# Layer 0's last two convolved blocks by seven half products in place of eight, with two row additions and one copy moved forward

## The chip, the core and the metric

The kernel runs on one core of a Trainium2 chip. The metric is device microseconds (us) of one execution. One core has five engines that run side by side and wait for each other by semaphores: TensorE (PE in the rows; its weight loads are PEld), VectorE (DVE), ScalarE (ACT), GpSimd (POOL) and SyncE (SP), which here only issues loads and stores; its issuing queue is SPq in the rows. Matrix products land in PSUM (`ps` in the rows, four slots of two banks here), and everything else on the chip lies in SBUF (`arena`, `resid`, `ring`, `small` and others).

## What is computed

Two layers of a hybrid backbone on 256 context and 512 latent tokens of width 1024. A layer mixes tokens (a bidirectional state-space scan, differential attention and latent attention share one input projection) and then runs 16 experts. The case touches the input projection of the scan in layer 0:

```python
for l in range(DEPTH):
    mod_l = split((silu_c @ ada_w[l] + ada_b[l]), N_MOD)
    h_l = modulate(rmsnorm(x, norm_mix_pre[l]), mod_l[0], mod_l[1])
    ...
    z, xbc, dt = split(h @ w_in, ...)       # xbc: 768 channels, six blocks of 128
    xbc = silu(centred_dwconv(xbc, conv_w, conv_b))           # 3 taps over tokens
    xs, bm, cm = split(xbc, [512, 640])     # blocks 0-3, block 4, block 5
    ...
    x = x + mod_l[5] * rmsnorm(expert_choice_ffn(...), norm_ffn_post[l])
```

`ada_w` gives rows of modulation. `xbc` has 768 channels, six blocks of 128: blocks 0 to 3 are `xs`, block 4 is `bm`, block 5 is `cm`. All is float32. Tokens number 768 in layer 0; in layer 1 block 5 is needed for the 512 latent tokens only.

## The kernel before

The program is written out engine by engine. `hT` holds the normed input, transposed: 8 slices of 128 features by 768 tokens. The six convolved blocks (`m` = 0 to 5) are made with channels on partitions, in PSUM jobs `conv_job(l, m)`.

**Plain blocks** (4 and 5): `feature_major` (lines 2468 to 2478; its products are L2476 in the rows) does 8 matmuls over the 8 feature slices for the first 512 tokens and 8 for the last 256. That is four half products each: two halves of the features by two halves of the tokens.

**Paired blocks** (0 with 1 and 2 with 3 in memory order of weights; pair `p` makes blocks `p` and `2 + p`): two blocks, two feature halves and two token halves are a 2 by 2 product of 2 by 2 blocks, done with seven half products in place of eight (`half_product`, lines 2861 to 2866, L2865 in the rows). One half product is four matmuls of 128 by 384. VectorE makes the sums that feed them: of tokens (`TH`), of weights (`SW`), and of the products, which it adds from PSUM into `E1`, `U3` and `CM` (`half_sum`, L1881; L1912 and L1933 are the sums that also free a PSUM slot). A product written twice into the same half bank must wait until its first value has been read: ScalarE copies it (`E1[p]`, L1304).

A float32 matmul shows as two records, so a half product is `x8` in the rows.

**Convolution.** For each block, in the order `CONV_ORDER = (2, 0, 3, 1, 4, 5)`, ScalarE scales by the middle tap and adds the bias (L1323, semaphore `conv_mid`), VectorE adds the two other taps with four instructions (L1987), and ScalarE applies SiLU (L1329, semaphore `xbc_ready`). Each engine takes the blocks strictly in that order. VectorE waits for all six before it multiplies block 4 by block 5 (L2002), and behind that product it copies the cumulative sums out of PSUM (L2007, L2008), which frees PSUM slot 3.

**TensorE after the paired blocks** (lines 2891 to 2920): block 4, the modulation rows `block_rows(l, 2, 2)` (L2508, 8 matmuls with the load of weights block 14), block 5, cumulative sums (L2900 to L2902), `block_rows(l, 2, 3)`, the turned sums `acT` (L2913, L2916), and then the gate product `z0` (L2923), whose PSUM slot is slot 3.

**Modulation rows.** `block_rows` leaves one block of 512 columns in PSUM; `rows_added` (line 1609) adds it to the rows so far and frees the slot: `rows_added(l, 2, 1)` stood behind convolved block 1, `rows_added(l, 2, 2)` behind block 4.

**Loads.** SyncE loads weight blocks of up to 2 MB into a ring of four slots, block `b` into slot `b % 4`. Its order is written out in line 822, and each load waits for the last use of the block that was in the slot (`block_used`, line 788):

```python
for b in [*range(10), 11, 10, 12, 13, 15, 14, *range(16, PRE_BLOCKS)]:
    ...
    if b >= RING and not (l and b - RING in EARLY):
        block_used(l, b - RING)
```

Block 10 has the weights of convolved blocks 0 to 3, block 15 those of blocks 4 and 5, blocks 12, 13, 14 and 16 the modulation rows `b` = 0 to 3 of part 2, block 17 those of the gate. For block 10, `block_used` waits until the last half product of the pairs is in PSUM (lines 804 to 810). Block 14 goes into the slot of block 10, so it is issued then. `block_rows(l, 2, 2)` waits for it (`arrived`, line 2463; semaphore `ring_full2`).

## Time and profile before

| | us |
|---|---|
| median of 3 runs | 2095.02 |
| lowest and highest of them | 2092.53, 2096.34 |
| the profiled execution, its own time | 2094.3 |
| its span, first to last instruction | 2092.2 |
| PE busy in it | 1942.3 (93%) |
| DVE, ACT, POOL busy | 721.6, 519.1, 186.9 |
| granted TensorE clock, mean | 0.988 of full speed |
| read from and written to HBM | 528.95 MB |

The profiled execution is 0.7 us below the median of the runs. Layer 0 mixes tokens until about 600 us of the span and runs its experts until about 1110 us; layer 1 does the same until about 1580 us and until the end. The six convolved blocks of layer 0 are made between 305 and 371 us. PE's busy time is modelled from its records and overlaps a little from row to row, so lengths of a stretch are best taken from start to start.

### The profile page before, as it was taken

Reading aid. Unit: us, or ns where it says so; the run is one execution under the profiler, and the core shown is the slowest. Engines: PE = TensorE matmul, PEld = TensorE weight load, DVE = VectorE, ACT = ScalarE, POOL = GpSimd, SP = SyncE. Lnnn points to the kernel's source line nnn. Section 1 sums busy time; section 2 is a strip of 40 time slices with the busy share of each in tenths; the row PEclk is TensorE's granted clock in tenths of the full one; section 3 lists DMA queues with packets and bytes.
Section 4 is the critical chain, followed back from the end, with each engine's and each line's share of the span. In section 5 each row is a group of like instructions: output and inputs, shape, how many; then the busy total and the mean of one; then the engine's idle time right before and its main releaser. Section 6 shows DMA issues by size and latency. Waiting matters only on the chain. (4 is left out here: it accounts for less than half of the span.)

```text
span 2092.2 us, 25952 instructions
## 1 busy us (share of the span) xinstructions
PE 1942.3 (93%) x10858; PEld 934.4 (45%) x10858; DVE 721.6 (34%) x1335; ACT 519.1 (25%) x1020; POOL 186.9 (9%) x216
## 2 busy tenths in 40 slices
PE   5998999989989999999999999999898998888886
PEld 2656565544433333333334866655445333232222
DVE  2258565372431110111113476563624111111113
ACT  4146552452300000000003255524321100000012
POOL 1300000120011111212012000001100000000000
PEclk9999999999999999999999999999999999999999
DMA  9520304222289999999999223024419999999996
GB/s 351 147 81 1 141 1 152 90 105 96 82 343 401 393 399 395 394 401 393 402 395 301 111 82 141 1 90 153 165 61 357 395 408 408 408 409 409 409 409 261
DMA packets 164805, 530.64 MB, mean 254 GB/s; under 512 B 11016, under 2 KB 19538, under 8 KB 164690
## 3 DMA queue, kind: packets, MB, share of 16 engines
q1 hardware_dynamic: 149344, 489.49, 60.0%
q0 software_dynamic: 15120, 39.43, 6.1%
q8 instruction: 87, 1.43, 0.3%
q14 instruction: 28, 0.23, 0.0%
q10 hardware_dynamic: 226, 0.07, 0.0%
HBM read 507.98 MB, written 20.97 MB: 253 GB/s over the span
## 5 line engine op out<-in xcount | busy, mean ns | idle before, releaser
L3267 PE MATMUL ps<-ring,arena 128*64 128x512 f32 x1040 | 233.2, 597 | 13.6 <-DMA ring<-in_w_up 8.8
L3267 PE MATMUL ps<-arena 128*64 128x512 f32 x720 | 165.0, 604 | 3.6 <-DMA arena<-in_w_gate 3.2
L3267 PEld LDWEIGHTS ps<-ring,arena 128*64 128x64 f32 x1040 | 72.1, 137 | 161.6 <-issue 141.3
L3093 PE MATMUL ps<-ring,arena 128*128 128x512 f32 x320 | 141.6, 597 | 1.0 <-ACT arena L1442 0.6
L2366 DVE TENSOR_TENSOR arena<-arena,ps 128x512 f32<-128x512 f32 x32 | 22.0, 688 | 280.1 <-ACT arena L1487 280.1
L3316 PE MATMUL ps<-ring,arena 128*64 128x512 f32 x496 | 112.4, 596 | 5.8 <-DMA ring<-in_w_down 5.8
L2476 PE MATMUL ps<-arena,ring 128*128 128x256 f32 (+1 forms) x384 | 110.4, 447 | 2.5 <-DMA ring<-in_w_in 2.5
L1487 ACT ACTIVATE arena<-ps 128x512 f32<-128x512 f32 x32 | 19.1, 597 | 373.4 <-PE ps L3267 373.4
L3316 PE MATMUL ps<-arena 128*64 128x512 f32 x432 | 97.9, 595 | 5.2 <-DMA arena<-in_w_down 4.5
L1066 ACT ACTIVATE arena<-ps 128x768 f32<-128x768 f32 (+6 forms) x111 | 79.9, 724 | 88.0 <-PE ps L2494 45.3
L3267 PEld LDWEIGHTS ps<-arena 128*64 128x64 f32 x720 | 50.4, 139 | 107.0 <-issue 100.3
L2476 PEld LDWEIGHTS ps<-arena,ring 128*128 128x128 f32 x384 | 73.2, 191 | 41.1 <-issue 31.5
L3093 PEld LDWEIGHTS ps<-ring,arena 128*128 128x128 f32 x320 | 59.7, 191 | 70.3 <-issue 69.5
L3216 PE MATMUL ps<-ring,arena 128*32 128x512 f32 x624 | 86.0, 594 | 0.4 <-DVE arena L2160 0.4
L2494 PE MATMUL ps<-const,arena 128*128 128x128 f32 x524 | 77.0, 283 | 7.9 <-DVE arena L1832 5.5
L1196 ACT ACTIVATE arena<-ps,nmax 128x768 f32<-128x768 f32 (+1 forms) x80 | 64.5, 811 | 60.6 <-DVE nmax L1715 56.1
L1715 DVE TENSOR_REDUCE nmax<-ps 128x1 f32<-128x768 f32 (+1 forms) x80 | 64.3, 846 | 39.8 <-PE ps L2682 38.9
L2494 PEld LDWEIGHTS ps<-const,arena 128*128 128x128 f32 x524 | 58.4, 143 | 42.5 <-issue 23.9
L2312 DVE TENSOR_TENSOR arena<-arena,ps 64x512 f32<-64x512 f32 x16 | 11.1, 692 | 188.7 <-ACT arena L1483 188.7
L2156 DVE TENSOR_TENSOR arena<-ps,coef 128x512 f32<-128x512 f32 (+1 forms) x48 | 28.8, 600 | 128.0 <-PE ps L3192 127.4
L3316 PEld LDWEIGHTS ps<-ring,arena 128*64 128x64 f32 x496 | 34.2, 137 | 77.3 <-issue 72.0
L914 POOL DMA_INDIRECT arena<-normed_rows,small x32 | 33.3, 1039 | 394.2 <-PE ps L3192 356.9
(417 smaller groups left out, 2821.8 us busy)
## 6 DMA issues: line engine op xcount, KB each, us to landing
ring<-in_w_up SPq DMA_DIRECT2D x33, 2048.0 KB, 14.7
ring<-in_w_gate SPq DMA_DIRECT2D x32, 2048.0 KB, 21.1
ring<-in_w_down SPq DMA_DIRECT2D x30, 2048.0 KB, 23.0
ring<-in_ada_w SPq DMA_DIRECT2D x24, 2048.0 KB, 9.9
arena<-in_w_down SPq DMA_DIRECT2D x19, 2048.0 KB, 23.2
arena<-in_w_gate SPq DMA_DIRECT2D x18, 2048.0 KB, 22.5
arena<-in_w_up SPq DMA_DIRECT2D x12, 2048.0 KB, 13.6
ring<-in_w_in SPq DMA_DIRECT2D x6, 2048.0 KB, 14.0
```

Of the source, the lines that this page charges most:

```text
L914: pool.indirect_dma_start(got_l[e % 2], None, halves_in, at_rows(e, 0)).then_inc(got_lat[e % 2], 16)
L1066: act.activation(dst, src, func, scale=scale).then_inc(*J.free(j))
L1196: act.activation(by_halves(PD[u % 2][m], t, nk // 2), by_halves(J.tile(j), t, 512), ACT.Exp, bias=nmax[:, c:c + 1], accum_out=esum[:, c:c ...
L1715: dve.tensor_reduce(nmax[:, c:c + 1], by_halves(J.tile(j), t, 512), AX_X if t < CT else AX_XY, ALU.max, negate=True).then_inc(S["negmax"], 1)
L2156: TT(x4, src.rearrange("p (c h n) -> p c h n", h=parts, n=n), cF[:, :, s].rearrange("p (h c) -> p c h", h=parts).unsqueeze(3) .to_broadcas ...
L2366: TT(hid_l, hid_l, px[0][:, 512:1024], ALU.mult).then_inc(S["hid_lat"], 1)
L2476: ins = mm(o[0:n, c0:c1], w[:, k, col:col + n], hT[:, k, c0:c1], start=k == 0, stop=k == KD - 1)
L2494: ins = pe.transpose(o[:, k * P:(k + 1) * P], src(k), ident)
L3093: ins = mm(o[:, hf * 512:(hf + 1) * 512], mix, wo[hf][:, k, :], start=k == 0, stop=k == KD - 1)
L3216: ins = mm(px[1][32 * i:32 * i + 32, 0:512], xc[e % 2][:, at:at + CAP_C], w[c][:, hf * 512:hf * 512 + 512], start=b + c == 0, stop=b * c == 3)
L3267: ins = mm(px[0][hf * 64:hf * 64 + 64, col:col + 512], xl[e % 2][:, at:at + CAP_L], w[c][:, hf * 512:hf * 512 + 512], start=b + c == 0, st ...
L3316: ins = mm(px[1][hf * 64:hf * 64 + 64, 512:1024], hT_l[0][:, at:at + CAP_L], w[c][:, hf * 512:hf * 512 + 512], start=b + c == 0, stop=b * ...
```

## The change

In layer 0 alone, blocks 4 and 5 are made as a third pair, by seven half products (`bc_product`). `CONV_ORDER` becomes a list per layer: in layer 0 block 5 now comes before block 4. VectorE makes four sums of weights (`bc_weight_sums`, before the last sum of block 1's pair) and seven sums of products (`bc_halves`, before the taps of block 5). ScalarE copies the first product (`E1[0]`) ahead of its work on block 1. TensorE does the first half product, then `block_rows(l, 2, 2)`, and then the other six. `rows_added(l, 2, 1)` moves forward to before the pairs' last sums in both layers, and in layer 0 `rows_added(l, 2, 2)` into `bc_halves`. SyncE's order stays as it was. The semaphore counts follow (33 sums and 15 products per layer).

```diff
@@ layout
-        CONV_ORDER = (2, 0, 3, 1, 4, 5)
+        CM += [CM[0], CM[2]]
+        CONV_ORDER = ((2, 0, 3, 1, 5, 4), (2, 0, 3, 1, 4, 5))
+        def last_pair_of_channels(x):
+            return SW[1 + x // 2][:, :, P * (x % 2):P * (x % 2) + P]
+        def plain(l, m):
+            return l > 0 and m >= 4
@@ ScalarE
+                    if l == 0 and m == 1:
+                        act.wait_ge(S["half_products"], products0 + 11)
+                        act.activation(E1[0], J.tile(conv_job(l, 4))[:, 0:HT], ACT.Copy).then_inc(S["half_out"], 1)
...
+                    elif m == 5:
+                        act.wait_ge(S["half_sums"], sums0 + 31)
                     else:
-                        act.wait_ge(*J.filled(j))
+                        act.wait_ge(*J.freed(conv_job(l, 5 if m == 4 else 2 * m + 1)))
@@ VectorE
+                rows_added(l, 2, 1)
                 early_half(0)
                 last_half(0)
+                def bc_weight_sums():
+                    n15 = block_base(l) + 15
+                    dve.wait_ge(ring_full[n15 % RING], ring_turns(n15) * 16)
+                    wb15, s_ = ringv(n15), [last_pair_of_channels(x) for x in range(4)]
+                    dve.wait_ge(*J.filled(conv_job(l, 2)))
+                    half_sum(s_[0], wb15[:, 0:4, P:2 * P], wb15[:, 4:8, P:2 * P], ALU.add)
+                    sums_done(21)
+                    half_sum(s_[1], s_[0], wb15[:, 0:4, 0:P], ALU.subtract)
+                    sums_done(22)
+                    half_sum(s_[2], wb15[:, 0:4, 0:P], wb15[:, 0:4, P:2 * P], ALU.subtract)
+                    half_sum(s_[3], wb15[:, 4:8, 0:P], s_[1], ALU.subtract)
+                def bc_halves():
+                    j0, j1 = conv_job(l, 4), conv_job(l, 5)
+                    dve.wait_ge(S["half_out"], out0 + 3)
+                    rows_added(l, 2, 2)
+                    dve.wait_ge(S["half_products"], products0 + 12)
+                    half_sum(CM[4][:, 0:HT], E1[0], J.tile(j0)[:, 0:HT], ALU.add)
+                    dve.wait_ge(S["half_products"], products0 + 13)
+                    half_sum(E1[0], E1[0], J.tile(j0)[:, 512:512 + HT], ALU.add)
+                    sums_done(28)
+                    dve.wait_ge(*J.filled(j0))
+                    TT(U3[0], E1[0], J.tile(j0)[:, 512:512 + HT], ALU.add).then_inc(*J.free(j0))
+                    dve.wait_ge(*J.freed(j0))
+                    half_sum(CM[5][:, HT:TOK], U3[0], J.tile(j1)[:, 0:HT], ALU.add)
+                    half_sum(E1[0], E1[0], J.tile(j1)[:, 0:HT], ALU.add)
+                    dve.wait_ge(S["half_products"], products0 + 15)
+                    half_sum(CM[5][:, 0:HT], U3[0], J.tile(j1)[:, 512:512 + HT], ALU.add)
+                    sums_done(30)
+                    dve.wait_ge(*J.filled(j1))
+                    TT(CM[4][:, HT:TOK], E1[0], J.tile(j1)[:, 0:HT], ALU.add).then_inc(*J.free(j1))
-                for m in CONV_ORDER:
+                for m in CONV_ORDER[l]:
...
                     if m == 3:
                         early_half(1)
+                        if l == 0:
+                            bc_weight_sums()
                         last_half(1)
+                    if m == 5 and l == 0:
+                        bc_halves()
...
-                    if m in (1, 4):
-                        rows_added(l, 2, m // 2 + (m == 1))
+                    if l and m == 4:
+                        rows_added(l, 2, 2)
@@ TensorE
                 w = arrived(wb + 15)
-                feature_major(conv_job(l, 4), w, 0, P)
-                block_rows(l, 2, 2)
-                feature_major(conv_job(l, 5), w, P, P, conv_start(l, 5) // P)
+                if l:
...
+                else:
+                    pe.wait_ge(*J.empty(conv_job(l, 4)))
+                    bc_product(0, 0, w[:, 0:4, 0:P], rows_half(0, 0)).then_inc(S["half_products"], 1)
+                    block_rows(l, 2, 2)
+                    pe.wait_ge(S["half_out"], out0 + 3)
+                    bc_product(0, 0, w[:, 4:8, 0:P], rows_half(4, 0)).then_inc(S["half_products"], 1)
+                    pe.wait_ge(S["half_sums"], sums0 + 24)
+                    bc_product(0, 1, last_pair_of_channels(1), TH[1]).then_inc(S["half_products"], 1)
+                    pe.wait_ge(*J.empty(conv_job(l, 5)))
+                    bc_product(1, 0, last_pair_of_channels(0), TH[0]).then_inc(S["half_products"], 1)
+                    pe.wait_ge(S["half_sums"], sums0 + 28)
+                    bc_product(0, 1, last_pair_of_channels(2), TH[2]).then_inc(*J.fill(conv_job(l, 4)))
+                    bc_product(1, 1, w[:, 4:8, P:2 * P], TH[3]).then_inc(S["half_products"], 1)
+                    pe.wait_ge(S["half_sums"], sums0 + 30)
+                    bc_product(1, 0, last_pair_of_channels(3), rows_half(4, 1)).then_inc(*J.fill(conv_job(l, 5)))
```

TensorE in layer 0, behind the last half product of the second pair, before the change (the row of 128x384 with `half_sums` ahead of it is that product; `ring,silu_c` rows are modulation rows; brackets name the semaphores waited for):

```order
L2865 MATMUL ps<-arena 128x384 [waits half_sums]
L2865 MATMUL ps<-arena 128x384 x3
L2476 MATMUL ps<-arena,ring 128x512 [waits ps_free0,ring_full3]
L2476 MATMUL ps<-arena,ring 128x512 x7
L2476 MATMUL ps<-arena,ring 128x256 x8
L2508 MATMUL ps<-ring,silu_c 32x512 [waits ring_full2,ps_free1]
L2508 MATMUL ps<-ring,silu_c 32x512 x7
L2476 MATMUL ps<-arena,ring 128x512 [waits ps_free2]
L2476 MATMUL ps<-arena,ring 128x512 x7
L2476 MATMUL ps<-arena,ring 128x256 x8
L2900 MATMUL ps<-small,const 128x48 [waits ps_free3,la_ready]
```

The same place with the change:

```order
L2954 MATMUL ps<-arena,ring 128x384 [waits ps_free0,ring_full3]
L2954 MATMUL ps<-arena,ring 128x384 x3
L2561 MATMUL ps<-ring,silu_c 32x512 [waits ring_full2,ps_free1]
L2561 MATMUL ps<-ring,silu_c 32x512 x7
L2954 MATMUL ps<-arena,ring 128x384 [waits half_out]
L2954 MATMUL ps<-arena,ring 128x384 x3
L2954 MATMUL ps<-arena 128x384 [waits half_sums]
L2954 MATMUL ps<-arena 128x384 x3
L2954 MATMUL ps<-arena 128x384 [waits ps_free2]
L2954 MATMUL ps<-arena 128x384 x3
L2954 MATMUL ps<-resid,arena 128x384 [waits half_sums]
L2954 MATMUL ps<-resid,arena 128x384 x3
```

The modulation rows of block 14 (`ring_full2`) now stand behind four matmuls of 128x384 where they stood behind sixteen, and six half products stand behind them.

VectorE from its last sum of products to the copies that free PSUM slot 3, with the change (`conv_mid` is ScalarE's middle tap; `xbc_ready` its last SiLU):

```order
L2021 TENSOR_TENSOR arena<-arena,ps 128x384 [waits ps_full2,half_sums]
L2040 SCALAR_TENSOR_TENSOR resid<-arena,par,resid 128x255 [waits conv_mid]
L2040 SCALAR_TENSOR_TENSOR resid<-arena,par,resid 128x511
L2040 SCALAR_TENSOR_TENSOR resid<-arena,par,resid 128x255 [waits dve_step]
L2040 SCALAR_TENSOR_TENSOR resid<-arena,par,resid 128x511
L2040 SCALAR_TENSOR_TENSOR resid<-arena,par,resid 128x255 [waits conv_mid]
L2040 SCALAR_TENSOR_TENSOR resid<-arena,par,resid 128x511
L2040 SCALAR_TENSOR_TENSOR resid<-arena,par,resid 128x255 [waits dve_step]
L2040 SCALAR_TENSOR_TENSOR resid<-arena,par,resid 128x511
L1632 TENSOR_TENSOR mod_rows<-ps,mod_rows 128x512 [waits half_used,ps_free1]
L2055 TENSOR_TENSOR arena<-resid 128x768 [waits xbc_ready]
L2060 COPY small<-ps 128x6x8 [waits ps_full3]
```

Before the change the taps of the last block alone stood between the last product and `xbc_ready`:

```order
L1615 TENSOR_TENSOR mod_rows<-ps,mod_rows 128x512 [waits ps_full1,ps_free1]
L1987 SCALAR_TENSOR_TENSOR resid<-ps,par,resid 128x255 [waits conv_mid]
L1987 SCALAR_TENSOR_TENSOR resid<-ps,par,resid 128x511
L1987 SCALAR_TENSOR_TENSOR resid<-ps,par,resid 128x255 [waits dve_step]
L1987 SCALAR_TENSOR_TENSOR resid<-ps,par,resid 128x511
L1618 TENSOR_TENSOR mod_rows<-ps,mod_rows 128x512 [waits half_used,ps_free1]
L2002 TENSOR_TENSOR arena<-resid 128x768 [waits xbc_ready]
L2007 COPY small<-ps 128x6x8 [waits ps_full3]
```

A last sum and the taps of a second block have come in ahead of the last block's taps.

ScalarE at the copy of the first product, with the change:

```order
L1337 ACTIVATE resid<-arena,par 128x768 [waits half_sums]
L1343 ACTIVATE resid<-resid 128x768 [waits half_sums]
L1326 ACTIVATE arena<-ps 128x384 [waits half_products]
L1337 ACTIVATE resid<-resid,par 128x768 [waits ps_free3]
L1343 ACTIVATE resid<-resid 128x768 [waits half_sums]
```

The copy stands behind the SiLU of block 3, which waits for that block's taps (`half_sums`), and ahead of block 1's middle tap.

## Rows read from the trace of the kernel before

**Rows 1.** Whole stages: us, PE busy, PEld, DVE, ACT, POOL busy, PEclk, DMA share, GB/s.

```profile
386.00:600.00 214.00, 198.85 (x963) 99.20 (x964) 105.16 (x208) 74.83 (x148) 26.31 (x33) 1.00 0.29 109
600.00:1110.00 510.00, 508.07 (x3564) 181.57 (x3566) 69.78 (x123) 38.13 (x61) 76.03 (x57) 1.00 1.02 393
1110.00:1580.00 470.00, 445.03 (x2491) 278.14 (x2490) 245.14 (x411) 192.06 (x385) 35.59 (x49) 0.98 0.33 120
1580.00:2093.00 513.00, 447.50 (x1889) 161.52 (x1887) 105.52 (x203) 51.86 (x88) 15.44 (x17) 0.98 0.98 389
```

**Rows 2.** PE's waits in layer 0's experts, 600 to 1110: total us, times, longest.

```profile
PE ps L3306 <- DVE arena L2366: 1.0, 1, 1.0
PE ps L3316 <- ACT arena L1517: 0.7, 1, 0.7
```

**Rows 3.** Timeline of PE, 330 to 400: start us, us, ..., [idle before <- releaser].

```profile
341.33 2.74 PE L2865 MATMUL ps<-arena 128*128 128x384 f32 x8
343.91 10.48 PE L2476 MATMUL ps<-arena,ring 128*128 128x512 f32 x32
354.32 1.92 PE L2508 MATMUL ps<-ring,silu_c 128*32 128x512 f32 x16
356.18 10.59 PE L2476 MATMUL ps<-arena,ring 128*128 128x512 f32 x32
366.60 0.32 PE L2900 MATMUL ps<-small,const 128*128 128x48 f32 x2
...
373.19 1.13 PE L2923 MATMUL ps<-ring,arena 128*128 128x512 f32 x2
```

**Rows 4.** Timeline of SyncE's DMA issues, 330 to 400.

```profile
344.10 0.99 SPq L835 DMA_DIRECT2D ring<-in_ada_w  x2
345.14 3.42 SPq L835 DMA_DIRECT2D ring<-in_w_in  x1
```

**Rows 5.** The load issued at 344.10, alone: from issue to landing.

```profile
DMA to landing us min/median/max: 7.8/7.8/7.8
```

**Rows 6.** Timeline of VectorE, 330 to 400.

```profile
343.31 0.55 DVE L1881 TENSOR_TENSOR arena<-arena,ps 128x384 f32<-128x384 f32 x1
...
345.22 2.33 DVE L1987 SCALAR_TENSOR_TENSOR resid<-arena,par,resid 128x255 f32<-128x255 f32 x4 [0.48 <-ACT resid L1323]
...
367.83 2.31 DVE L1987 SCALAR_TENSOR_TENSOR resid<-ps,par,resid 128x255 f32<-128x255 f32 x4 [9.46 <-ACT resid L1323]
...
371.05 0.96 DVE L2002 TENSOR_TENSOR arena<-resid 128x768 f32<-128x768 f32 x1 [0.31 <-ACT resid L1329]
...
372.16 0.25 DVE L2008 COPY small<-ps 128x96 f32<-128x96 f32 x1
...
387.31 3.70 DVE L2023 TENSOR_TENSOR arena<-arena 128x512 f32<-128x512 f32 x6
```

**Rows 7.** Timeline of ScalarE, 330 to 400.

```profile
347.57 0.84 ACT L1329 ACTIVATE resid<-resid 128x768 f32<-128x768 f32 x1 [2.39 <-DVE resid L1987]
...
366.80 0.99 ACT L1323 ACTIVATE resid<-ps,par 128x768 f32<-128x768 f32 x1 [8.15 <-PE ps L2476]
370.18 0.84 ACT L1329 ACTIVATE resid<-resid 128x768 f32<-128x768 f32 x1 [2.38 <-DVE resid L1987]
```

**Rows 8.** Timeline of ScalarE, 300 to 332: a copy of half a product.

```profile
308.60 0.49 ACT L1304 ACTIVATE arena<-ps 128x384 f32<-128x384 f32 x1 [4.44 <-PE ps L2865]
```

**Rows 9.** Timeline of PE, 10 to 30: row-block products after waits for their loads.

```profile
18.96 3.52 PE L2508 MATMUL ps<-ring,silu_c 128*32 128x512 f32 x16 [6.06 <-DMA ring<-in_ada_w]
24.39 1.92 PE L2508 MATMUL ps<-ring,silu_c 128*32 128x512 f32 x16 [1.91 <-DMA ring<-in_ada_w]
```

**Rows 10.** Timeline of PE, 386 to 620 and 1425 to 1530: the longer waits.

```profile
589.96 0.40 PE L3176 MATMUL ps<-const,arena 32*128 32x32 f32 x4 [2.33 <-ACT arena L1468]
...
1450.75 1.14 PE L2971 MATMUL ps<-resid 32*128 32x512 f32 x8 [2.13 <-issue]
```

**Rows 11.** The 8 us behind that last wait, columns as in rows 1.

```profile
1452.00:1460.00 8.00, 8.00 (x32) 4.91 (x36) 4.54 (x5) 2.46 (x3) 2.08 (x2) 0.57 0.00 0
```

More of the change, by code:

```diff
@@ L1300, in _ @@
                     act.wait_ge(s_xst, 16 * nq)
-                products0, sums0 = 10 * l, 22 * l
+                products0, sums0 = 15 * l, 33 * l
                 for p in range(2):
@@ L1312, in _ @@
                 act.activation(dts[1], dts[1], ACT.Ln).then_inc(S["dt_log"], 1)
-                for i, m in enumerate(CONV_ORDER):
+                for i, m in enumerate(CONV_ORDER[l]):
                     j = conv_job(l, m)
-                    if m in (2, 3):
+                    if l == 0 and m == 1:
+                        act.wait_ge(S["half_products"], products0 + 11)
+                        act.activation(E1[0], J.tile(conv_job(l, 4))[:, 0:HT], ACT.Copy).then_inc(S["half_out"], 1)
+                    if plain(l, m):
+                        act.wait_ge(*J.filled(j))
+                    elif m in (2, 3):
                         act.wait_ge(S["half_sums"], sums0 + (15, 20)[m - 2])
-                    elif m < 2:
-                        act.wait_ge(*J.freed(conv_job(l, 2 * m + 1)))
+                    elif m == 5:
+                        act.wait_ge(S["half_sums"], sums0 + 31)
                     else:
-                        act.wait_ge(*J.filled(j))
+                        act.wait_ge(*J.freed(conv_job(l, 5 if m == 4 else 2 * m + 1)))
                     on = slice(conv_start(l, m), TOK)
-                    src = CM[m] if m < 4 else J.tile(j)
+                    src = J.tile(j) if plain(l, m) else CM[m]
                     act.activation(XB[:, m, on], src[:, on], ACT.Identity, bias=pc[:, R_CB + m:R_CB + m + 1],
                                    scale=pc[:, R_CW + CONV_T + m:R_CW + CONV_T + m + 1]).then_inc(S["conv_mid"], 1)
-                    if m < 4:
-                        act.wait_ge(S["half_sums"], sums0 + (16, 19, 21, 22)[i])
+                    if not plain(l, m):
+                        act.wait_ge(S["half_sums"], sums0 + (16, 19, 25, 26, 32, 33)[i] - (0 if l == 0 or i < 2 else 4))
                     else:
@@ L1865, in _ @@
                     dve.wait_ge(s_xst, 16 * nq)
[L1866 removed]
+                sums0, out0, products0 = 33 * l, 3 * l, 15 * l
                 n10 = block_base(l) + 10
@@ L1979, in _ @@
                         early_half(1)
+                        if l == 0:
+                            bc_weight_sums()
                         last_half(1)
+                    if m == 5 and l == 0:
+                        bc_halves()
                     dve.wait_ge(*v.next(S["conv_mid"]))
-                    src, dst = CM[m] if m < 4 else J.tile(j), XB[:, m, :]
+                    src, dst = J.tile(j) if plain(l, m) else CM[m], XB[:, m, :]
                     for tap, sh in ((0, -1), (2, 1)):
@@ L1991, in _ @@
                             dve.wait_ge(*v.next(dve_step))
-                    if m < 4:
+                    if not plain(l, m):
                         ins.then_inc(S["half_sums"], 1)
@@ L2850, in _ @@
                 w = arrived(wb + 10)
-                sums0, out0 = 22 * l, 2 * l
+                sums0, out0 = 33 * l, 3 * l
                 def weight(p, half, k0):
@@ L2891, in _, with bc_product @@
                 w = arrived(wb + 15)
-                feature_major(conv_job(l, 4), w, 0, P)
-                block_rows(l, 2, 2)
-                feature_major(conv_job(l, 5), w, P, P, conv_start(l, 5) // P)
+                if l:
+                    feature_major(conv_job(l, 4), w, 0, P)
+                    block_rows(l, 2, 2)
+                    feature_major(conv_job(l, 5), w, P, P, conv_start(l, 5) // P)
+                else:
+                    def bc_product(i, hf, a, b):
+                        o = J.tile(conv_job(l, 4 + i))[:, 512 * hf:512 * hf + HT]
+                        for k in range(4):
+                            ins = mm(o, a[:, k, :], b[:, k, :], start=k == 0, stop=k == 3)
+                        return ins
+                    pe.wait_ge(*J.empty(conv_job(l, 4)))
+                    bc_product(0, 0, w[:, 0:4, 0:P], rows_half(0, 0)).then_inc(S["half_products"], 1)
+                    block_rows(l, 2, 2)
+                    pe.wait_ge(S["half_out"], out0 + 3)
[9 more added lines that the diff above has]
+                    bc_product(1, 0, last_pair_of_channels(3), rows_half(4, 1)).then_inc(*J.fill(conv_job(l, 5)))
                 pe.wait_ge(*w_.next(S["la_ready"]))
```

1 line of the change is left out of this document (removed).

## The prediction

> **What bounds the kernel.** I read the table of stages first. From 600 to 1110 us, layer 0's experts, PE is busy 508 of 510 us [rows 1], and its two longest waits there are 1.0 and 0.7 us, for VectorE and ScalarE, none for a load [rows 2]: PE bounds that stage. While layer 0 mixes, from 386 to 600, PE is busy 199 of 214 us with the DMA engines at 0.29 [rows 1], so PE and its short waits for its neighbours bound that one too. Layer 1 mixes in the same way, and its experts have the DMA engines at 0.98 [rows 1]. Every load of the later stages waits for a slot that PE frees, so a shift of PE in layer 0 moves the loads behind it as well. I found no place behind 387 us that waits for something earlier than PE's own work, and so take it that what PE gains or loses here reaches the end in full.
>
> Then the timelines of PE, SyncE, VectorE and ScalarE around the blocks. PE goes through the stretch without a gap: the last half product of the pairs from 341.33 to 343.91, block 4 to 354.32, modulation rows to 356.18, block 5 to 366.60, and small products until the gate product at 373.19 [rows 3].
>
> **What is saved.** A half product takes 2.58 us (341.33 to 343.91). Blocks 4 and 5 took 10.41 and 10.42 us, 20.83 together [rows 3]. Seven half products take 7 x 2.58 = 18.06. PE does **2.8 us** less work, all of it on the path.
>
> **The load.** Where PE now does the modulation rows decides more. They begin at 354.32 today, behind sixteen matmuls. With the change they stand behind one half product, so PE comes to them at 343.91 + 2.58 = 346.49. They need weights block 14, and SyncE issues it when the pairs' last product is done, at 344.10 [rows 4], into the slot that this product's weights had. It lands 7.8 us after its issue [rows 5], at 351.9. The change leaves SyncE's order and that condition alone. Today the load has 2.4 us to spare; with the change PE stands idle from 346.5 to 351.9, **5.4 us**, and the six other half products are queued behind.
>
> **The copy and the weight sums** are hidden by that same wait. Four sums of 128x512 on VectorE cost 0.62 us each by the rows of 128x512 (six in 3.70, [rows 6]), 2.5 us together. They come ahead of block 3's taps, which move from 345.22 to about 343.31 + 0.48 + 2.5 + 0.47 = 346.8. Those take 2.33, ScalarE's SiLU 0.84 [rows 6, 7], the copy 0.49 [rows 8]: the copy ends at about 350.4, 1.5 us before the load lands. Without the load's wait, PE would stand until 350.4 in place of 346.49 + 1.86 = 348.35: 2.0 us. The other sums of `bc_halves` (0.5 us each, by 343.31) fall each beside a half product of 2.58 us and hold nobody, nor do the two additions of modulation rows: the first falls into idle time of VectorE, and the second has its product long before its slot is wanted.
>
> **The tail.** PE ends its seventh product at 351.9 + 1.86 + 6 x 2.58 = 369.2, against 366.60: 2.6 us later (5.4 less 2.8). Today the chain behind block 5 is middle tap at 366.80 (0.99), VectorE's taps (2.31), SiLU at 370.18, the product at 371.05 and the copies to 372.16 + 0.25 = 372.4 [rows 6, 7]. That frees the slot for the gate product at 373.19, 0.8 us early. With the change the last product completes block 4, and VectorE, which goes in order, does the last sum (0.55), block 5's taps (2.31), ScalarE block 5's SiLU (0.84) and only then block 4's middle tap; from there all is as before. The chain is 0.55 + 2.31 + 0.84 = 3.7 us longer. Less the 0.8 us that it had to spare, PE waits **2.9 us** ahead of the gate product.
>
> Everything behind waits for PE's gate product, eight microseconds long. The sum without the clock is 5.4 - 2.8 + 2.9 = **+5.5 us**.
>
> **The clock.** The granted clock is 1.00 in all of layer 0 from 386 on [rows 1]; both new waits could take it to the lower of its levels, 1.2 in place of 2.4 GHz. The rows have cases on both sides. The same sixteen records of modulation rows took 3.52 us after a wait of 6.06 us for their load and 1.92 after one of 1.91 [rows 9]: 1.6 us lost. A wait of 2.33 us at 589.96 left the clock at 1.00 through its stage, one of 2.13 us at 1450.75 was followed by 8 us at 0.57 [rows 10, 11], 8 x 0.43 = 3.4 us lost. So each wait can cost 0 to 3.4 us. The first, of 5.4 us, is nearest to the 6.06 and the same work follows: I take 1.6. The second, 2.9 us, lies between: I take half of that, 0.8. The Trainium skill ("TensorE: Matmul & The Clock Gate", Part 1: The HAM clock gate) says that the low clock is the default and that activity releases it, so that a gap brings it back; it speaks against this change. By the page the sum would be 5.5 + 1.6 + 0.8 = 7.9, without it 5.5; rows 9 agree with it.
>
> The sum is **+7.9 us**: 2094.3 + 7.9 = 2102.2 for an execution like the profiled one. That one lies 0.7 below the median of the runs, so I expect a median of **2103 us**, 0.4% slower.
>
> **The rivals.** A measurement of this kernel tells 0.2%, 4.2 us, from no change.
>
> (a) *The load does not bind.* If block 14 is there earlier than its row says, the copy binds in its place from 350.4: PE loses 2.0, saves 2.8, and waits 2.9 at the gate: +2.1 us, about 2097, no change that can be told. For it speaks that three loads of 2 MB are issued together and this one's 7.8 us could be shorter alone; against it that it was issued first. It decides from a landing before 348.5. Chance 0.08.
>
> (b) *The saving shows, on the other side.* One mechanism: VectorE's and ScalarE's tail is hidden behind the small products and the gate waits for nobody. It would need the load before 346.5, and the last SiLU to start by about 368.2 where its present start is 370.18, so that slot 3 is free for PE at 370.4. Then PE's 2.8 us reach the end: 2092 us, not slower. Against it stand the order on VectorE and the issue at 344.10. Chance 0.03.
>
> (c) *Given back later.* PE waits a good 15 us between 386 and 600 [rows 1]. If some of these waits end on engines or loads that the shift does not move, they shrink, and of 5.5 us 2 or 3 remain: 2097 to 2098. For it speaks that 15 us are a lot; against it that GpSimd, ScalarE and VectorE there work on what PE has just made. Chance 0.10.
>
> (d) *The clock falls for long at both waits*, 3.4 us each: 5.5 + 6.8 = +12.3, 2107. Chance 0.07, slower as well.
>
> (e) *It does not do what it says*: a count that makes the plain path run on, or an order of waits that costs a lot more than 10 us. The written order of PE shows the seven products. Chance 0.02.
>
> The forecast itself, +4.2 to +10, has 0.70.
>
> **How the numbers follow.** Slower by over 0.2%: forecast 0.70, (d) 0.07 and half of (e), 0.78. Within 0.2%: (a), most of (c) and most of (b), 0.20. Faster by over 0.2%: the saving is 2.8 us, so it would need something that I do not see, 0.02. The range begins at 2097.5, which takes in most of (c) and the forecast without any loss of clock less the scatter of the runs (they lie 2.5 us below to 1.3 above their median); it ends at 2107.5 with (d).
>
> **What would show it.** In PE's timeline of the changed kernel: one half product at 344, then a wait of 5 to 5.5 us for the load into `ring` ahead of the modulation rows at about 352, which take nearer 3.5 than 1.9 us; the copy on ScalarE at about 350, before that; six half products without a gap; then the gate product at about 379 to 381 behind a wait of about 3 us for VectorE's copies. From there to the end every landmark is later by one and the same 6 to 9 us. The prediction is wrong if the modulation rows begin before 350, if the gate product begins before 376, or if the shift at the start of the experts is much smaller than at the gate product.

## The result, and the profile after

| | before | after |
|---|---|---|
| median, us (runs) | 2095.42 (8) | 2104.78 (8) |
| lowest to highest, us | 2092.53 to 2097.60 | 2101.83 to 2109.03 |
| ratio after to before, 95% interval | | 1.0048 (1.0039 to 1.0058) |
| profiled execution, us; its span | 2094.3; 2092.2 | 2102.89; 2100.8 |
| mean granted clock over the runs of after | | 0.985 |

The change makes the kernel slower by 0.48% (0.39 to 0.58%); between the medians it is 9.4 us, or 0.45%. (Here and below the ratio with its interval is an estimate from all the runs, and can differ from the quotient of the two medians by up to 0.0004.) The forecast was 2103, range 2097.5 to 2107.5.

The timeline of TensorE in the profile of after, 330 to 405 us (columns as in rows 3; `L2954` is `bc_product`, `L2561` `block_rows`, `L2999` the gate product):

```profile
340.86 2.74 PE L2918 MATMUL ps<-arena 128*128 128x384 f32 x8
343.44 2.74 PE L2954 MATMUL ps<-arena,ring 128*128 128x384 f32 x8
351.67 3.61 PE L2561 MATMUL ps<-ring,silu_c 128*32 128x512 f32 x16 [5.49 <-DMA ring<-in_ada_w]
355.21 2.85 PE L2954 MATMUL ps<-arena,ring 128*128 128x384 f32 x8
357.89 5.32 PE L2954 MATMUL ps<-arena 128*128 128x384 f32 x16
363.06 2.74 PE L2954 MATMUL ps<-resid,arena 128*128 128x384 f32 x8
365.63 2.74 PE L2954 MATMUL ps<-arena,ring 128*128 128x384 f32 x8
368.21 2.74 PE L2954 MATMUL ps<-arena 128*128 128x384 f32 x8
370.80 0.32 PE L2976 MATMUL ps<-small,const 128*128 128x48 f32 x2
...
380.43 1.10 PE L2999 MATMUL ps<-ring,arena 128*128 128x512 f32 x2 [2.98 <-DVE small L2061]
```

Where rows 3 have no gap, two waits stand: 5.49 us for the load ahead of the modulation rows, and 2.98 us for VectorE's copies ahead of the gate product. The seven half products are there and take 2.58 us each from start to start, but for the one behind the modulation rows (2.68). The modulation rows take 3.61 us in place of 1.92.

The load was issued at the same place as before. SyncE's issue, and that load alone from issue to landing:

```profile
343.63 0.99 SPq L844 DMA_DIRECT2D ring<-in_ada_w  x2
```

```profile
DMA to landing us min/median/max: 7.9/7.9/7.9
```

343.63 + 7.9 = 351.5, and the modulation rows begin at 351.67. Their other condition, the PSUM slot that the moved addition frees (semaphore `ps_free1`), was met long before, at 333.5:

```profile
332.78 0.68 DVE L1629 TENSOR_TENSOR mod_rows<-ps,mod_rows 128x512 f32<-128x512 f32 x1
```

ScalarE in the same stretch (the copy of the first product is L1326, the middle tap L1337, SiLU L1343):

```profile
348.78 0.84 ACT L1343 ACTIVATE resid<-resid 128x768 f32<-128x768 f32 x1 [4.05 <-DVE resid L2040]
349.53 0.47 ACT L1326 ACTIVATE arena<-ps 128x384 f32<-128x384 f32 x1
...
374.64 1.02 ACT L1337 ACTIVATE resid<-arena,par 128x768 f32<-128x768 f32 x1
378.05 0.84 ACT L1343 ACTIVATE resid<-resid 128x768 f32<-128x768 f32 x1 [2.39 <-DVE resid L2040]
```

VectorE: one of the four weight sums, then the tail, from the last sum (L2021) over the taps of blocks 5 and 4 (L2040) to the copies that free slot 3:

```profile
343.31 0.68 DVE L1895 TENSOR_TENSOR arena<-ring 128x512 f32<-128x512 f32 x1
...
371.06 0.56 DVE L2021 TENSOR_TENSOR arena<-arena,ps 128x384 f32<-128x384 f32 x1 [2.09 <-PE ps L2954]
371.54 2.32 DVE L2040 SCALAR_TENSOR_TENSOR resid<-arena,par,resid 128x255 f32<-128x255 f32 x4
375.69 2.33 DVE L2040 SCALAR_TENSOR_TENSOR resid<-arena,par,resid 128x255 f32<-128x255 f32 x4 [1.83 <-ACT resid L1337]
...
380.03 0.25 DVE L2061 COPY small<-ps 128x96 f32<-128x96 f32 x1
```

The copy ends at 350.0, 1.5 us before the load has landed. From the end of TensorE's last half product (370.80) to the end of the copies (380.28) it is 9.5 us; before it was 5.8 (366.60 to 372.41, [rows 3, 6]). The difference is the 3.7 us of a sum, a block's taps and a SiLU.

Later landmarks. Execution by execution the whole program lies a little earlier or later already at 340 us, so I count from the first product behind the second pair: 343.91 before [rows 3], 343.44 after. The gate product lies 29.28 us behind it before and 36.99 after: **+7.7 us**. The experts of layer 0 begin at 601.66 before, and here:

```profile
478.14 0.60 PE L3206 MATMUL ps<-arena,const 16*128 16x32 f32 x2 [1.92 <-ACT arena L1441]
...
609.96 7.09 PE L3343 MATMUL ps<-ring,arena 128*64 128x512 f32 x32 [0.21 <-DVE arena L2213]
```

That is 257.75 before and 266.52 after, +8.8 us. The 1.1 us that came in between has its place behind 478 us, after a wait of 1.92 us:

```profile
348.00:356.00 8.00, 4.33 (x19) 1.20 (x20) 3.60 (x7) 2.98 (x4) 0.00 (x0) 0.57 1.05 391
...
476.00:484.00 8.00, 6.08 (x26) 4.33 (x23) 2.11 (x4) 2.16 (x6) 3.25 (x6) 0.79 1.02 409
```

(Stretches of the profile of after, columns as in rows 1.) The granted clock is 0.57 around the wait for the load and 0.79 in the later stretch, where the profile of before stood at 1.00: in 348 to 356 by its own row of that stretch, and from 386 on by rows 1.

### The profile page after: what moved, and what is told of

Its sections match the earlier page's. It is cut to its first block and busy times, and to the rows that moved or that the text cites. A ratio compares the mean times of both kernels' runs of the same rounds, so it can differ in the third digit from the quotient of the medians.

```text
span 2100.8 us, 25951 instructions
## 1 busy us (share of the span) xinstructions
PE 1945.5 (93%) x10850; PEld 934.3 (44%) x10850; DVE 727.8 (35%) x1346; ACT 520.1 (25%) x1021; POOL 187.4 (9%) x216
## 5 line engine op out<-in xcount | busy, mean ns | idle before, releaser
L2529 PE MATMUL ps<-arena,ring 128*128 128x256 f32 (+1 forms) x320 | 89.1, 438 | 2.2 <-DMA ring<-in_w_in 2.2
L2529 PEld LDWEIGHTS ps<-arena,ring 128*128 128x128 f32 x320 | 61.2, 192 | 31.1 <-issue 22.2
```

The costliest lines, as they stand in the source:

```text
L2529: ins = mm(o[0:n, c0:c1], w[:, k, col:col + n], hT[:, k, c0:c1], start=k == 0, stop=k == KD - 1)
```

## The experiments

The theory: the loss is a wait for a load whose issue the change did not move, a longer chain of taps behind the last product, and a clock that falls in these waits. The rivals: the copy or the weight sums hold PE and not the load; the moved additions cost something; the clock plays no part; the scheme of seven products costs this much in any order.

Each set of runs had runs of the kernel before on the same chip. "Gate product" is its distance from the first product behind the second pair in the profiled execution, against the 29.28 us of before; "experts" is the same for the start of layer 0's experts, against 257.75. (In e2, whose rows come first, both are counted from the end of the pairs, 342.12.) "Clock" is the mean granted clock over the executions; before's was 0.9883 beside e2 to e5, 0.9876 beside e1 and e6 to e8, and 0.9875 beside e9 to e11.

| kernel | gate product, us | experts, us | time of this, before, us | ratio (95%) | clock |
|---|---|---|---|---|---|
| the change | +7.7 | +8.8 | 2104.78, 2095.42 | 1.0048 (1.0039 to 1.0058) | 0.9848 |
| e1_additions | 0.0 | +2.5 | 2096.72, 2095.81 | 1.0001 (0.9991 to 1.0010) | 0.9875 |
| e2_rows_first | +10.0 | +15.3 | 2107.21, 2094.64 | 1.0063 (1.0046 to 1.0080) | 0.9842 |
| e3_rows_later | +6.1 | +13.1 | 2110.29, 2094.64 | 1.0078 (1.0061 to 1.0094) | 0.9812 |
| e4_early_copy | +7.8 | +9.2 | 2107.74, 2094.64 | 1.0066 (1.0049 to 1.0083) | 0.9840 |
| e5_filled | +6.0 | +9.3 | 2104.51, 2094.64 | 1.0051 (1.0034 to 1.0068) | 0.9865 |
| e6_early_sums_out | +5.4 | +6.1 | 2098.89, 2095.81 | 1.0013 (1.0003 to 1.0023) | 0.9868 |
| e7_no_waits | +0.5 | +6.0 | 2100.74, 2095.81 | 1.0024 (1.0015 to 1.0034) | 0.9851 |
| e8_no_waits_sums_out | -2.6 | -1.1 | 2094.57, 2095.81 | 0.9995 (0.9986 to 1.0004) | 0.9865 |
| e9_filled_gate | +0.5 | +2.3 | 2098.28, 2095.85 | 1.0011 (1.0002 to 1.0020) | 0.9872 |
| e10_no_waits_sums_out | -2.6 | +1.7 | 2095.18, 2095.85 | 0.9993 (0.9984 to 1.0002) | 0.9860 |
| e11_both_filled | +6.1 | +9.8 | 2102.49, 2095.85 | 1.0029 (1.0018 to 1.0040) | 0.9876 |

**e1, the moved addition alone.** The kernel before with

```diff
+                rows_added(l, 2, 1)
                 early_half(0)
...
-                    if m in (1, 4):
-                        rows_added(l, 2, m // 2 + (m == 1))
+                    if m == 4:
+                        rows_added(l, 2, 2)
```

> The kernel before, with the addition of modulation rows (2, 1) moved forward in both layers and nothing else. Theory: it falls into idle time of VectorE (0.5 us, then 2 us more behind the next sum), so 0 within the scatter, and the gate product of layer 0 begins when it did. Rival (a moved addition holds up the pairs' last sums and through them PE): up to +1.4 us, 0.7 a layer.

No difference, in the time or at the gate product: where it was moved to, the addition is free. But its profiled execution has two stretches at a lower clock further on, and so begins the experts 2.5 us later than before's, though nothing else was changed:

```profile
432.00:440.00 8.00, 6.58 (x29) 3.03 (x29) 6.29 (x9) 4.00 (x7) 2.04 (x2) 0.79 0.01 2
472.00:480.00 8.00, 7.78 (x25) 5.17 (x26) 1.92 (x2) 0.28 (x2) 1.39 (x3) 0.79 1.02 408
```

The profiled execution of before has 1.00 in both. So what a single profile gains or loses between the gate product and the experts can be scatter, by 2.5 us at least; the profiles are compared below at the gate product.

**e2, the rows first, without a third pair.** The kernel before with the modulation rows ahead of plain block 4, in layer 0:

```diff
+                if l == 0:
+                    block_rows(l, 2, 2)
                 feature_major(conv_job(l, 4), w, 0, P)
-                block_rows(l, 2, 2)
+                if l:
+                    block_rows(l, 2, 2)
```

> The kernel before, with the modulation rows of block 14 put ahead of plain block 4 in layer 0 and nothing else. Theory (the load's issue at 344.1 and its 7.8 us set when the rows can begin): PE stands idle about 8 us from the end of the pairs, the rows begin at about 352, and every later landmark moves by +8 us, and by 1 to 3.4 us more if the clock falls: +8 to +11. Rival (the wait of the change is for ScalarE's copy or VectorE's sums, not for the load): neither exists here, so no wait and no change of time, 0.

TensorE in it, SyncE's issue of the load and its landing, and VectorE's addition of the modulation rows before:

```profile
350.61 3.56 PE L2508 MATMUL ps<-ring,silu_c 128*32 128x512 f32 x16 [8.33 <-DVE mod_rows L1615]
```

```profile
342.31 0.99 SPq L835 DMA_DIRECT2D ring<-in_ada_w  x2
```

```profile
DMA to landing us min/median/max: 8.1/8.1/8.1
```

```profile
349.83 0.68 DVE L1615 TENSOR_TENSOR mod_rows<-ps,mod_rows 128x512 f32<-128x512 f32 x1
```

The pairs end at 342.1, the load is issued at 342.31 and lands at 350.4, and PE begins at 350.61. But the row names VectorE's addition as what ended the wait, and rightly: it frees the PSUM slot that the rows need, it still stands behind block 1's taps here, and it ends at 350.51. The two conditions are met within 0.1 us of each other, so e2 cannot tell them apart and does not show the load's wait by itself. It refutes its rival, since with no copy and no weight sum in it the kernel waits 8.3 us. It also shows what the moved addition is for. At its old place it holds the rows as long as the load does here, and in the change it would have held them longer: block 1's taps end there at 353.3, so that by my estimate (no run has it) the addition would have ended at about 353.9, 2.4 us behind the load.

The kernel loses 10.0 us at the gate product: the wait and 1.6 us in the modulation rows, which take 3.56. That is within the 8 to 11 expected, but the whole time rose by 12.6, beyond it.

**e4, the copy earlier.** The change with the copy moved ahead of block 3's SiLU, behind its middle tap:

```diff
-                    if l == 0 and m == 1:
-                        act.wait_ge(S["half_products"], products0 + 11)
-                        act.activation(E1[0], J.tile(conv_job(l, 4))[:, 0:HT], ACT.Copy).then_inc(S["half_out"], 1)
                     if plain(l, m):
...
                                    scale=pc[:, R_CW + CONV_T + m:R_CW + CONV_T + m + 1]).then_inc(S["conv_mid"], 1)
+                    if l == 0 and m == 3:
+                        act.wait_ge(S["half_products"], products0 + 11)
+                        act.activation(E1[0], J.tile(conv_job(l, 4))[:, 0:HT], ACT.Copy).then_inc(S["half_out"], 1)
```

> The change, with the copy of the first product ahead of block 3's SiLU on ScalarE, so that it ends at about 346.9 in place of 350.0. Theory (the load binds until 351.7, the copy is hidden): no gain, rows still begin at 351.7, +8 to +9.5 us against before as the change. Rival (the copy binds): the time falls by 3 us, to +6.

ScalarE's copy and TensorE's modulation rows:

```profile
346.59 0.49 ACT L1338 ACTIVATE arena<-ps 128x384 f32<-128x384 f32 x1 [1.50 <-PE ps L2954]
```

```profile
351.95 3.64 PE L2561 MATMUL ps<-ring,silu_c 128*32 128x512 f32 x16 [5.40 <-DMA ring<-in_ada_w]
```

The copy is there 4.9 us before the rows begin, and nothing is gained: +7.8 at the gate product. The time is +13.1 us, where +8 to +9.5 was expected; its interval overlaps the change's (1.0049 to 1.0083, 1.0039 to 1.0058) and excludes the rival's +6. The copy does not bind beside the load. Why the median lies 3.7 us above the change's is not shown; its profiled execution is the fastest of its four and has, as the change's, falls of the clock in layer 0 at the load's wait and near 478 alone.

**e3, the rows later.** The change with the modulation rows behind the third half product and their addition one sum later:

```diff
                     bc_product(0, 0, w[:, 0:4, 0:P], rows_half(0, 0)).then_inc(S["half_products"], 1)
-                    block_rows(l, 2, 2)
...
                     bc_product(0, 1, last_pair_of_channels(1), TH[1]).then_inc(S["half_products"], 1)
+                    block_rows(l, 2, 2)
```

> The change, with the modulation rows two half products later (behind the third) and their addition on VectorE one sum later. Theory: the load no longer binds; PE goes through one product and then waits until the copy ends at about 350.0 (3.9 us), has the load when it comes to the rows, and ends the seventh product at about 367.4 in place of 370.8; the wait of 3.0 us before the gate product stays. Against before: +4.2 us without a fall of the clock, up to +6 with one. Rival (the load is not the cause, the seven products with their sums cost this much anyway): the same +9 us as the change.

TensorE in it:

```profile
351.93 4.31 PE L2954 MATMUL ps<-arena,ring 128*128 128x384 f32 x8 [3.86 <-ACT arena L1326]
...
380.65 1.10 PE L2999 MATMUL ps<-ring,arena 128*128 128x512 f32 x2 [2.97 <-DVE small L2061]
381.73 1.59 PE L2999 MATMUL ps<-ring,arena 128*128 128x512 f32 x2
383.39 2.06 PE L2999 MATMUL ps<-ring,arena 128*128 128x512 f32 x2
```

The wait for the load is gone and the next one shows, the 3.86 us for the copy that I had worked out. But the clock fell in both places (4.31 us for a half product of 2.74, 2.06 for matmuls of 1.10): +6.1 at the gate product where +4.2 was expected without a fall. The whole time missed by far: +15.7 us where up to +6 was expected. The mean clock of its executions is the lowest of all. Beyond its two waits the profile shows the lower clock in three more places between the gate product and the experts (from about 444, 481 and 604 us). At the experts it is +13.1, so 7.0 us came in on that stretch. This says where the time went; why this kernel falls most often stays open.

**e5, the wait filled.** The change with two half products of no use while the load is awaited, written where the third product overwrites them:

```diff
+                    for _ in range(2):
+                        bc_product(0, 1, w[:, 0:4, 0:P], rows_half(0, 0))
                     block_rows(l, 2, 2)
```

> The change, with two more half products of no use (the first product's operands, into a half bank that the third product overwrites) while PE waits for the load. It adds 5.2 us of work to PE. Theory (PE stands idle for the load, and the idle time also takes the clock down): the rows begin at the same 351.7, now after a wait of 0.3 us, the clock stays at 1.00, the rows take 1.9 in place of 3.6 us and all behind is 1.9 us earlier: +6 to +7 against before. Rival (the clock plays no part): the same +9. Rival (PE was not idle there): 5 us slower than the change.

TensorE in it:

```profile
343.87 7.90 PE L2954 MATMUL ps<-arena,ring 128*128 128x384 f32 x24
352.10 1.92 PE L2561 MATMUL ps<-ring,silu_c 128*32 128x512 f32 x16 [0.33 <-DMA ring<-in_ada_w]
...
379.16 1.10 PE L3001 MATMUL ps<-ring,arena 128*128 128x512 f32 x2 [2.97 <-DVE small L2061]
380.29 2.05 PE L3001 MATMUL ps<-ring,arena 128*128 128x512 f32 x2
```

With 5.2 us more work on PE the rows begin at the same distance, take 1.92 us, and the gate product is 1.7 us earlier than in the change. So PE was idle, and the idle time itself cost 1.7 us of clock. Then the clock falls behind the second wait, which in the change's profiled execution it did not. In the time it does not show: +9.9 against the +6 to +7 expected, and against the change's +9.4. The second wait, still open here, is filled in e11.

**e6, the sums out earlier.** The change with the copies of the cumulative sums ahead of block 4's taps in layer 0:

```diff
                     if m == 5 and l == 0:
                         bc_halves()
+                    if m == 4 and l == 0:
+                        sums_out()
...
+                if l:
+                    sums_out()
                 j = jb("cum")
-                dve.wait_ge(*J.filled(j))
...
```

> The change, with VectorE's copies of the cumulative sums (which free PSUM slot 3) ahead of block 4's taps in layer 0, where they stood behind the last SiLU. Theory (the tail holds PE by that slot): the wait of 3.0 us ahead of the gate product is gone, the gate product begins at about 377.3 in place of 380.4, 3 us less than the change at every later landmark: +5 to +6.5 against before. Rival (PE, or what follows, waits for the last SiLU in another place): the 3 us come back behind the gate product, no gain, +8 to +9.

TensorE's modulation rows, the end of the seven products and the gate product, in its timeline, and the landing of the load, which was issued at 345.25:

```profile
353.79 3.64 PE L2569 MATMUL ps<-ring,silu_c 128*32 128x512 f32 x16 [5.99 <-DMA ring<-in_ada_w]
...
370.58 2.74 PE L2962 MATMUL ps<-arena 128*128 128x384 f32 x8
...
379.75 1.13 PE L3007 MATMUL ps<-ring,arena 128*128 128x512 f32 x2
```

```profile
DMA to landing us min/median/max: 8.4/8.4/8.4
```

The wait of 3 us is gone; PE comes to the gate product straight from the turned sums. It is 2.3 us nearer than in the change, because this execution's load landed 0.5 us later (a wait of 5.99). One small one takes its place: between the first two pairs of matmuls of the gate product PE now waits for VectorE's last addition of modulation rows, which stands behind block 4's taps, so that the second pair starts 1.54 us behind the first where before it was 1.10. That gives 0.4 us back. The late landing also tells what the rows wait for: here they begin 0.1 us behind it (345.25 + 8.4 = 353.65, 353.79), and in the change, e4 and e5, with landings at 351.5, 351.8 and 352.0, they begin at 351.67, 351.95 and 352.10. The rows move with the load.

The time is +3.1 where +5 to +6.5 was expected: 6.3 us came back and not 3. The mean clock rose with it (0.9868 against 0.9848). In the profiled executions the clock had not fallen at this wait in the change, so these two profiles do not show where the other 3 us were.

**e7, no wait within the seven products.** The modulation rows behind the first four products and their addition as in e3, the copy as in e4, and the fourth product, which needs no copy, second:

```diff
                     bc_product(0, 0, w[:, 0:4, 0:P], rows_half(0, 0)).then_inc(S["half_products"], 1)
+                    pe.wait_ge(S["half_sums"], sums0 + 21)
+                    pe.wait_ge(*J.empty(conv_job(l, 5)))
+                    bc_product(1, 0, last_pair_of_channels(0), TH[0]).then_inc(S["half_products"], 1)
...
```

> The change, with three moves: the fourth product second (it needs no copy), the modulation rows behind the first four products, the copy ahead of block 3's SiLU. Theory: no wait of PE from 343 to the end of the seven products, which come at about 363.4 in place of 370.8; the 3.0 us ahead of the gate product stay, since the tail of taps is as long as before: gate product 0.3 us later than in the kernel before, +0.3 us, no difference that can be measured. Rival (without the waits the saving of 2.8 us shows): -2.8.

The last of the products and the gate product:

```profile
361.51 2.74 PE L2954 MATMUL ps<-arena 128*128 128x384 f32 x8
...
373.74 2.04 PE L3000 MATMUL ps<-ring,arena 128*128 128x512 f32 x2 [2.99 <-DVE small L2061]
375.86 1.75 PE L3000 MATMUL ps<-ring,arena 128*128 128x512 f32 x2
```

From 343.98 to 364.1 PE has no gap, and the gate product lies at +0.5 (expected +0.3). What the seven products save, the longer tail takes back. The time is +4.9 and not +0.3. The profiled execution shows where its own 6.0 us at the experts came in: 1.7 at the gate product, which runs at the lower clock, 2.6 behind the wait at 473 and 1.2 behind the one at 595.

**e9, the gate's wait filled.** e7 with one useless half product inside the 3.0 us, into the slot that the turned sums then overwrite:

```diff
+                    if l == 0 and at == 8:
+                        for k in range(4):
+                            mm(o[:, 0:HT], hT[:, k, 0:P], hT[:, k, 0:HT], start=k == 0, stop=k == 3)
                     for t in range(NT):
```

> The kernel of e7_no_waits with one half product of no use on PE ahead of the second set of turned sums (into a slot that they overwrite), inside the 3.0 us in which PE waits before the gate product. Theory (that wait itself costs 0.5 us, and what e7 lost beyond it is the clock that falls behind the wait): the gate product begins at the same distance from the first product as in e7 (29.8 us), after a wait of 0.4 us, runs at the full clock, and the time is 1.6 to 3 us below e7's: +2 to +3.5 against before. Rival (the rest of e7's loss has its cause elsewhere): the same +4.9.

```profile
367.47 2.85 PE L2988 MATMUL ps<-arena 128*128 128x384 f32 x8
...
373.21 1.10 PE L3003 MATMUL ps<-ring,arena 128*128 128x512 f32 x2
```

(Its timeline of TensorE.) The gate product lies where it did, and runs at the full clock. The useless product delays the turned sums behind it, so that they fill the wait. The median falls from +4.9 to +2.4 us for work that does nothing, as expected; each was measured against before on its own chip, and the two intervals overlap (1.0015 to 1.0034, 1.0002 to 1.0020).

**e11, both waits filled.** The change with the fillers of e5 and e9:

> The change with useless half products in both of its waits, two while the load is awaited and one before the gate product. Theory: neither wait takes the clock down any more; the gate product begins 6.0 us later than in the kernel before (5.5 - 2.8 + 2.9 and the longer chain of sums, no clock in it), and the time is +6 to +7: of the change's 9.4 us, 2.5 to 3.5 were the clock. Rival (the clock plays no part in the change's loss): +9.

```profile
352.12 1.92 PE L2561 MATMUL ps<-ring,silu_c 128*32 128x512 f32 x16 [0.35 <-DMA ring<-in_ada_w]
...
379.19 1.10 PE L3004 MATMUL ps<-ring,arena 128*128 128x512 f32 x2
```

(Its timeline of TensorE.) +6.1 us at the gate product and +6.6 us in the time, and the mean clock of its executions is that of before, 0.9876 and 0.9875. Its interval (1.0018 to 1.0040) and the change's (1.0039 to 1.0058) all but part. This splits the change's 9.4 us: about 6 are waits, less the saved product, and about 3 are clock that those waits take down.

**e8 and e10, the version without the two costs.** e7 with the copies of e6, run in two sets:

> The last two together: no wait within the seven products, and the copies of the cumulative sums ahead of block 4's taps. Theory: both costs of the change are gone and the saving is left: the gate product 2.8 us earlier than in the kernel before, and so the end, -2.8 us (0.13%). Rival (the chain of taps still holds PE later, at the products that turn the convolved blocks): between 0 and -2.8, with a wait of PE behind the gate product for the last SiLU.

> e8_no_waits_sums_out once more, beside the others of this set on the same chip. Theory: the gate product 2.6 us earlier than before, and a time 0 to 3 us below before's, 1 us on average, as in e8. Rival: no gain at all, the saving of 2.8 us is lost in every execution in stages behind.

```profile
370.29 1.13 PE L3008 MATMUL ps<-ring,arena 128*128 128x512 f32 x2
...
384.28 0.49 PE L3042 MATMUL ps<-resid 64*128 64x128 f32 x4 [0.79 <-ACT arena L1075]
```

(e8's timeline of TensorE.) The gate product is 2.6 us earlier than before in both sets, and the longer of the waits behind it is the 0.8 us for ScalarE that the kernel before has too; the 0.4 us within the gate product that e6 showed stand ahead of it, so that 2.2 us are left behind that wait (384.28 - 343.59 = 40.69; before, 386.75 - 343.91 = 42.84). So the saving of the seventh product exists, and most of it can be had on PE's path. In the time both sets lie below before, by 1.2 and 0.7 us, and each interval holds 1: it beats the change clearly, and before by nothing that is shown. The mean clock is lower (0.9865 and 0.9860 against 0.9876 and 0.9875), and the profiled executions show places: e8's has one lower stretch, 0.79 in 468 to 476, and is at -1.1 at the experts; e10's has two, 0.58 in 468 to 476 and 0.79 in 588 to 596, and is at +1.7. Whether this kernel falls there more often than before, of which one execution was profiled, and why it should, stays open.

e8 against e7, on one chip, repeats e6 against the change: with the second wait gone the gate product is 3.1 us earlier and the median 6.2 us lower, where e9, which fills the wait and keeps it, gives 2.5. So at the median this wait costs its 3 us and about as much again, of which e9 shows 2.5 to be clock, as far as intervals that overlap can.

## Why the prediction was right

By its own steps, at the gate product of the profiled execution:

| step | predicted, us | measured, us |
|---|---|---|
| work saved, two plain blocks to seven half products | -2.8 | -2.8 (seven in 18.1) |
| wait for block 14's load | +5.4 | +5.49 |
| wait ahead of the gate product | +2.9 | +2.98 |
| clock at the first wait | +1.6 (0 to 3.4) | +1.8 (rows 3.61 for 1.92, next product 0.1) |
| clock at the second wait | +0.8 (0 to 3.4) | 0 in this execution; about 1.7 in e7's |
| sum, at the gate product | +7.9 | +7.7 |
| to the end, profiled execution | +7.9 | +8.6 (counted from the first product, +9.1) |
| to the end, medians | +8 | +9.4 |

The measured steps add up to 7.5; the other 0.2 lies mostly in the first wait, which is 5.65 us when it is taken from start to start, since a row's end is modelled 0.16 us late.

The load was the main term. The rows begin when it lands, in four profiled executions with different landings (e6); e4 rules the copy out, and e3 shows it as the next one behind, as worked out. e2 does not show it by itself. The four weight sums took 2.65 us from start to start (343.31 to 345.96) where 2.5 was taken, without effect, and the moved addition of rows (2, 1) cost nothing (e1); the one of rows (2, 2) was not tried by itself. The tail is shown by e6, which takes only its hold on PE away, and by e7, in which it is the one cost left.

The terms that were sized by choice were those of the clock, and their ground was thinner than it looks. The 1.6 us came from rows 9, where the modulation rows took 3.52 us behind a wait of 6.06, but the granted clock is 1.00 there:

```profile
20.00:22.00 2.00, 2.00 (x15) 0.23 (x6) 0.00 (x0) 1.97 (x4) 0.00 (x0) 1.00 1.05 386
```

So rows 9 do not show that the clock made them slow, and no run shows what did; the change's own rows do (3.61 us at a clock of 0.57 in 348 to 356), and the size is nearly the same. Half of a fall at the second wait was fair: of the five profiled executions with that wait (the change, e3, e4, e5, e7), three show the fall at the gate product and two do not, so at this length one profile does not tell. The Trainium skill ("TensorE: Matmul & The Clock Gate", Part 1: The HAM clock gate) says that activity releases the clock and a gap brings it down. e5, e9 and e11 agree: useless products in the gap, no fall at that place. What the prediction left out is that falls also come behind shorter waits in the stages behind, here 1.9 us at 478; this is the 1.1 us between +7.7 and +8.8. It took the one profiled execution of before, with 1.00 in all of layer 0 from 386 on, for the rule, and e1's execution shows falls on that stretch in a kernel without the third pair. That the sum and the end agree so well is in part luck: the 0.8 us set down for the second wait did not come in this execution, and 1.1 us came elsewhere. At the medians the change costs 9.4 us, 1.5 more than the sum. With both waits filled 6.6 are left where the sum without the clock had 5.5 (e11), so 2.8 us go to what the two waits do to the clock, where the sum had 2.4.

Of the rivals, (a) falls with the landing at 351.5, (b) with the two waits, (c) with +8.8 at the start of the experts: nothing was given back. (d) falls with 1.8 us of clock at the first wait and none at the second, in place of 3.4 at each, and (e) with the seven products in the rows. Rival (b) is also what e8 builds by hand, and even there it stays within what can be measured, as its 2.8 us said.

## What to carry to other kernels

Before an instruction is moved forward, look up when the load that it needs is issued and what that issue waits for: here the condition was the end of the step just before it, so all the cover that the load had was the sixteen matmuls that were taken from between them. When one step of a chain is made the last of two (block 4's taps behind block 5's), look for what is released behind the chain and could be released before it; moving three small copies took away a wait of 3 us. When something must move forward, look at everything that it waits for: here the addition that frees its PSUM slot had to move with it (e2). A saving of 2.8 us does not pay for a wait of 3.0 us that also takes the clock down (e7).

## What the runs showed that I had not expected

A wait can cost more than its length. One half product that computes nothing, put into a wait of 3.0 us, lowered the median by 2.5 us (e9 against e7, intervals that overlap), such products in both waits brought the change from +9.4 to +6.6 (e11), and taking the wait of 3.0 us away gave back about 6 us both times (e6, e8). And the scatter of one kernel's executions follows the granted clock: of the change's eight, the three slowest (2108 to 2109 us) have 0.983, the fastest 2101.83 has 0.987.
